# Residual kept with tokens on partitions from the convolution's output on

## The reference, cut to what matters

```python
for i in range(2):
    m = short_conv_mixer(x, ...) if i == 0 else dsa_mixer(x, ...)   # both end in  (...) @ w_out
    x = layer_norm(ALPHA * x + m, ln1_g[i], ln1_b[i])               # over the 1024 features of a token
    f = hier_moe(x, ...)     # top group, top 2 of 8 experts in it: 64 experts of 1024 x 256 (x2) and 256 x 1024
    x = layer_norm(ALPHA * x + f, ln2_g[i], ln2_b[i])
def layer_norm(x, g, b):
    mu = mean(x); var = mean(square(x - mu))
    return (x - mu) * rsqrt(var + 1e-5) * g + b
```

## Time and profile before

| what | value |
|---|---|
| three timed runs | 3143.69, 3145.0, 3147.49 us |
| the profiled execution | span 3143.2 us (the page gives the span and no other time for it) |
| PE, PEld busy | 2787.1 us (89%), 2133.7 us (68%) |
| DVE, ACT, POOL busy | 1063.2 us (34%), 707.9 us (23%), 108.9 us (3%) |
| chain that ended last | PE 70%, DMA 21%, DVE 4%, ACT 2% |
| HBM | 189 GB/s over the span |

### The profile page before, as it was taken

How to read it: one execution, slowest core, us unless ns; L and a number is a source line. 1 busy time by engine, 2 the same in 40 slices (tenths; PEclk the granted TensorE clock), 3 DMA queues, 4 the chain that set the end, 5 groups by cost and what they waited for, 6 DMA issues and landing times.

```text
span 3143.2 us, 51582 instructions
## 1 busy us (share of the span) xinstructions
PE 2787.1 (89%) x21208; PEld 2133.7 (68%) x21208; DVE 1063.2 (34%) x2168; ACT 707.9 (23%) x1224; POOL 108.9 (3%) x175
## 2 busy tenths in 40 slices
PE   6999999999899999996887887889999868878787
PEld 6888874755688888875666666754577656666666
DVE  4554642222522254435211111229155341111113
ACT  3212330143322243212100000112264310000012
POOL 0000001000000000000000000000000000000000
PEclk8999999999999999996999999989999879999998
DMA  6655333211223222320499999641100209999980
GB/s 229 190 184 184 134 103 107 81 54 54 81 84 104 94 93 80 108 94 1 196 422 422 422 422 422 255 152 52 67 1 27 81 27 400 422 422 422 422 369 27
DMA packets 205503, 590.07 MB, mean 188 GB/s; under 512 B 9264, under 2 KB 133360, under 8 KB 156000
## 3 DMA queue, kind: packets, MB, share of 16 engines
q1 hardware_dynamic: 202832, 575.47, 47.7%
q0 software_dynamic: 2288, 12.39, 1.2%
q10 hardware_dynamic: 288, 0.89, 0.1%
HBM read 586.58 MB, written 7.38 MB: 189 GB/s over the span
## 4 chain that ended last, share of the span: by engine, by line
PE 70%; DMA 21%; DVE 4%; ACT 2%; issue 2%; SPq 1%; DVEq 0%; ACTq 0%
PE bank L1638 33%; DMA ring<-in_exp_w 20%; PE bank L1945 8%; PE bank L2020 4%; PE bank L1791 4%; PE bank L1760 3%; PE bank L1919 2%; PE bank L2005 2%; PE bank L1597 2%; PE bank L1749 1%; PE bank L1578 1%; SPq L453 1%; PE bank L1839 1%; PE bank L1612 1%; PE bank L2109 1%
## 5 line engine op out<-in xcount | busy, mean ns | idle before, releaser
L1638 PE MATMUL bank<-parts 128*128 128x512 f32 x3008 | 937.3, 393 | 29.4 <-DVE parts L998 17.3
L1638 PEld LDWEIGHTS bank<-parts 128*128 128x128 f32 x3008 | 566.9, 190 | 149.3 <-issue 28.9
L1945 PE MATMUL bank<-ring,arena 128*64 128x256 f32 x4096 | 496.6, 393 | 178.8 <-DMA ring<-in_exp_w 178.1
L1638 PE MATMUL bank<-parts,ring_low 128*128 128x512 f32 x1504 | 588.6, 391 | 0.0
L1945 PEld LDWEIGHTS bank<-ring,arena 128*64 128x64 f32 x4096 | 329.4, 135 | 309.4 <-issue 203.6
L1638 PEld LDWEIGHTS bank<-parts,ring_low 128*128 128x128 f32 x1504 | 284.8, 189 | 59.9
L992 DVE TENSOR_TENSOR ring_low<-ring,parts 128x2048 fp32r<-128x2048 f32 x96 | 215.2, 2245 | 196.5 <-ACT parts L645 196.2
L1963 PEld LDWEIGHTS bank<-arena,ring 128*64 128x64 f32 x8192 | 266.2, 138 | 16.4 <-ACT arena L623 1.1
L1407 DVE SCALAR_TENSOR_TENSOR arena<-arena,bank 128x128 f32<-128x128 f32 x128 | 44.2, 346 | 656.3 <-ACT arena L765 656.3
L1963 PE MATMUL bank<-arena,ring 128*64 128x64 f32 x8192 | 263.3, 222 | 0.7 <-ACT arena L623 0.7
L645 ACT ACTIVATE parts<-ring 128x2048 fp32r<-128x2048 f32 x96 | 179.9, 1873 | 233.9 <-DMA ring<-in_w_ffn_in 109.3
(11 more groups left out here) (290 smaller groups left out, 2467.0 us busy)
## 6 DMA issues: line engine op xcount, KB each, us to landing
ring<-in_exp_w SPq DMA_DIRECT2D x384, 1024.0 KB, 10.3
ring<-in_w_ffn_in SPq DMA_DIRECT2D x44, 1024.0 KB, 5.9
ring<-in_w_ada SPq DMA_DIRECT2D x36, 1024.0 KB, 5.3
ring<-in_w_ffn_out SPq DMA_DIRECT2D x20, 1024.0 KB, 5.1
ring<-in_w_in SPq DMA_DIRECT2D x18, 1024.0 KB, 5.1
ring<-in_conv_w_in SPq DMA_DIRECT2D x12, 1024.0 KB, 5.1
ring<-in_attn_w_in SPq DMA_DIRECT2D x10, 1024.0 KB, 9.6
ring<-in_attn_w_out SPq DMA_DIRECT2D x8, 1024.0 KB, 5.0
```

The costliest lines, as they stand in the source:

```text
L1638: i = mm(o, a[:, cols[0], cols[1]], b, start=first_ and n == 0, stop=last_ and n == 2)
L1945: x = mm(bank[s][64 * f:64 * f + 64, 0:2 * P].rearrange("p (w n) -> p w n", w=2), XW[:, s, k], ring[:, 3 * s:3 * s + 2, c0:c0 + 2 * P - 1: ...
```

## The change

From the output product of the convolution on, the residual is `HT`, the same memory as `H` but read as `[128 tokens, 4 token tiles, 1024 features]`.

- **Residual turned.** During the convolution PE transposes `U` into two spare banks, four transposes after each of the 8 convolution tiles (`residual`), and ACT copies each group into `HT`.
- **Output products** (`token_output`, for `conv_out` and `dsa_out`): the activation tile is now the stationary operand and 512 columns of the weight the moving one. PE waits for whole chunks. In the second half the last two chunks are taken together, for one token tile after the other, so that bank `4 + t` is finished for `t = 0..3`.
- **Slot sum**: `SWT` stationary, the slot results moving; 4 token tiles for each half of the features.
- **Layer norm** by token tile on DVE (`bn_stats` on each half of 512, `bn_aggr`, reciprocal, one subtract-and-multiply over 1024) and ACT (root). Then PE turns the tile back to features (`turn_tokens`), and ACT and DVE apply gain and bias while they copy it out of the banks into `U` (`lifted`). The router's logits follow for each tile. The old products with ones, the squares, `to_tokens` and their waits are gone.
- **Gain and bias of the residual itself** are applied later, by POOL: `HT * g` and `+ b` over `[128, 1024]`, eight instructions after the last expert window, or in the attention's projections; rows `g` and `b` are broadcast over partitions by DMAs of POOL. The gather carries them for the experts in ACT's copy (`Identity` with scale and bias).
- **Low part `XTL`**: four instructions of 1024, placed after the router's weights and before the wait for the ranks.
- **Fourth layer norm**: DVE applies gain and bias itself and SP stores each token tile by its own DMA.

```diff
+            for d in range(KT):                                   # ACT, in the convolution
...
+                if d:
+                    residual(d - 1)
...
+            residual(7)
             out_high("conv_out", KT, lambda k: BC[:, k], UP, lambda k: conv_ready(k))
...
+            def token_output(name, kts, x, turn, logits):         # PE
+                def product(half, c, k, t):
...
+                        last = mm(bank[4 * half + t][:], a[:, at, P * t:P * t + P], b[:, k - 4 * c, :],
+                                  start=(k == m == 0), stop=(k == kts - 1 and m == 2))
+                for half, c in [(0, c) for c in range(n)] + [(1, c) for c in range(n - 2)]:
+                    ready(half, c)
...
+                for c in (n - 2, n - 1):
+                    ready(1, c)
+                for t in range(TT):
+                    for c in (n - 2, n - 1):
...
+                    if t >= 1:
+                        turn(t - 1)
+                    if t >= 2:
+                        logits(t - 2)
+                logits(2)
+                turn(3)
+                logits(3)
...
+                def tokens_back(half, t):                         # PE, slot sum
+                    if half:
+                        pe.wait_ge(sem("ht"), 8 * (1 + 2 * l) + t + 1)
+                    for s in range(8):
+                        for j, part in enumerate((YSH, YSL)):
+                            x = mm(bank[4 + t][:], SWT[:, s, P * t:P * t + P], part[half][:, s],
...
+                for t in range(TT):
+                    tokens_back(1, t)
+                    if l == 0 and t:
+                        turn_tokens(1, t - 1)
...
+            def deep_add(j, t, half, src):                        # DVE
+                STT(out=h, in0=h, scalar=ALPHA, in1=src, op0=ALU.mult, op1=ALU.add).then_inc(sem("ht"), 1)
+                dve.wait_ge(sem("ht"), n)
+                st.did(nc.vector.bn_stats(BNS[:, t, 6 * half:6 * half + 6], h))
+            def normal(j, t):
+                dve.wait_ge(sem("sd"), 4 * j + t + 1)
+                seq(nc.vector.reciprocal(RS[:, t:t + 1], SD[:, t:t + 1]))
+                TSc(HT[:, t], HT[:, t], MV[:, t, 0:1], RS[:, t:t + 1], ALU.subtract, ALU.mult).then_inc(sem("xn"), 1)
+            def layer_norm(j, second_half):
+                for t in range(TT):
+                    second_half(t)
+                    moments(j, t)
+                    if j == 3:
...
+                        stored(j, t)
+                        continue
+                    if t:
+                        lifted(j, t - 1)
+                    normal(j, t)
+                if j < 3:
+                    lifted(j, 3)
...
+                for n, v in enumerate((layer, 2 + layer) + ((5, 7) if layer else ())):   # POOL, before the windows
+                    pool.dma_start(ROWS[:, n], lnrows[v].partition_broadcast(P)).then_inc(sem("ln_vectors"), 16)
...
+                pool.wait_ge(sem("ln_vectors"), 160 if layer else 64)                    # POOL, after them
+                for t in range(TT):
+                    st.did(pool.tensor_tensor(HT[:, t], HT[:, t], ROWS[:, 0], ALU.mult))
...
+                    pool.wait_ge(sem("ht"), 16)                   # POOL, layer 0
+                    pool.dma_start(ROW2, lnrows[4].partition_broadcast(P)).then_inc(sem("ln_vectors"), 16)
                     pool.dma_start(BKT[0:BUCKETS], ...)           # and rel_bias, scratch, spread, TOE as before
...
+                    pool.wait_ge(sem("ln_vectors"), 80)
+                    pool.wait_ge(sem("lt"), 16)
+                    for t in range(TT):
+                        st.did(pool.tensor_tensor(HT[:, t], HT[:, t], ROW2, ALU.mult))
+                    st.wait()
+                    pool.dma_start(ROW2, lnrows[6].partition_broadcast(P)).then_inc(sem("ln_vectors"), 16)
+                    pool.wait_ge(sem("ln_vectors"), 96)
+                    for t in range(TT):
+                        pool.tensor_tensor(HT[:, t], HT[:, t], ROW2, ALU.add).then_inc(sem("resid"), 1)
...
-            out_low("dsa_out", HEADS2, lambda k: Q2[:, k], UP, lambda: deep_out("dsa_out", 4, 0))
-            deep_out("dsa_out", 4, 1)
-            norm(6, 3, lambda k: col("ln1_g", 8 + k))
+            dve.wait_ge(sem("resid"), 8)
+            out_low("dsa_out", HEADS2, lambda k: Q2[:, k], UP, lambda: deep_out("dsa_out", 4, 2, 0), half_at=6)
+            layer_norm(2, lambda t: deep_out("dsa_out", 4, 2, 1, (t,)))
...
+            for t in range(TT):
+                sp.wait_ge(sem("final"), t + 1)
+                sp.dma_start(out[0, P * t:P * t + P], HT[:, t]).then_inc(sem("stored"), 16)
```

More of the change, by code:

```diff
@@ L757, in moe @@
                     c, k = g // 8, g % 8
-                    evac(XST[:, k, 512 * c:512 * c + 512], bank[g % 4][:], "moe_xst")
+                    A_(XST[:, k, 512 * c:512 * c + 512], bank[g % 4][:], ACT.Identity, scale=gpart[:, l, k:k + 1],
+                       bias=gpart[:, 2 + l, k:k + 1]).then_inc(sem("moe_xst"), 1)
                 act.wait_ge(sem("moe_plan"), l + 1)
@@ L853, in _ @@
             weights_high(split_at["ffn1"] + 1)
[L854 removed]
+            norm(2, lambda k: mod[:, 48 + k:49 + k], True)
             ffn(1)
@@ L865, in conv_ready, with residual @@
                     act.wait_ge(sem("conv_b"), 8)
+            def residual(g):
+                act.wait_ge(sem("side_tp"), g + 2)
+                evac(HT[:, g // 2, 512 * (g % 2):512 * (g % 2) + 512], bank[6 + g % 2][:], "side_out")
             for d in range(KT):
@@ L1027, in roots, with norm @@
                     TSc(diag[:, t], ident, small[:, 52 + t:53 + t], None, ALU.mult).then_inc(sem("diag"), 1)
-            def norm(i, ln, gain, parts_of=None, shift=None):
-                if ln:
-                    dve.wait_ge(sem("mean"), ln)
-                    for k in range(KT):
-                        STT(out=H[:, k], in0=bank[2][:], scalar=-1.0 / D, in1=H[:, k],
-                            op0=ALU.mult, op1=ALU.add).then_inc(sem("centred"), 1)
+            def norm(i, gain, parts_of=None, shift=None):
                 if i:
@@ L1266, in _, with deep_out @@
                     weights_low(split_at["conv"] + 3 * (d // 2 + 1) + 2)
[L1267 to L1274 removed]
+            def deep_out(name, n, j, half, tiles=range(TT)):
+                for t in tiles:
+                    bank_ready(name, n, half, t)
+                    deep_add(j, t, half, bank[4 * half + t][:])
+            out_low("conv_out", KT, lambda k: BC[:, k], UP, lambda: None)
+            dve.wait_ge(sem("side_out"), 9)
+            deep_out("conv_out", 2, 0, 0)
+            layer_norm(0, lambda t: deep_out("conv_out", 2, 0, 1, (t,)))
             def moe(l):
[L1277 to L1279 removed]
                 dve.wait_ge(sem("rows"), 16 * 12)
@@ L1437, in moe, with token_half @@
                     rest(g)
-                for d in range(KT):
-                    if d < 4:
-                        rest(8 + 2 * d)
-                        rest(9 + 2 * d)
-                    dve.wait_ge(sem("moe_f"), 8 * l + d + 1)
-                    deep_add(d, bank[4 + d % 4][:])
+                def token_half(t, half):
+                    dve.wait_ge(sem("moe_f"), 8 * l + 4 * half + t + 1)
+                    deep_add(1 + 2 * l, t, half, bank[4 + t][:])
+                for t in range(TT):
+                    rest(8 + 2 * t)
+                    rest(9 + 2 * t)
+                    dve.wait_ge(sem("resid"), 8 * l + t + 1)
+                    token_half(t, 0)
+                layer_norm(1 + 2 * l, lambda t: token_half(t, 1))
             moe(0)
-            norm(5, 2, lambda k: col("ln2_g", k))
             dve.wait_ge(sem("vb_mm"), 1)
@@ L1606, in rstd, with norm @@
                 x.then_inc(sem("rstd"), 1)
-            def norm(i, ln):
-                if ln:
-                    for k in range(KT):
-                        pe.wait_ge(sem("h"), 8 * (i - 1) + max(k + 1, 4))
-                        x = mm(bank[2][:], ones[:], H[:, k], start=(k == 0), stop=(k == KT - 1))
-                    x.then_inc(sem("mean"), 1)
-                for k in range(KT) if ln else range(5, KT):
+            def norm(i):
+                for k in range(5, KT):
                     sums(i, k, k == 0, "squares", 8 * (i - 1) + k + 1)
@@ new lines, in turn_tokens @@
+            def turn_tokens(j, t):
+                pe.wait_ge(sem("xn"), 4 * j + t + 1)
+                if j == 1 and t >= 2:
+                    pe.wait_ge(sem("u_low"), 4 * j + t - 1)
+                    pe.wait_ge(sem("u_high"), 4 * j + t - 1)
+                for h in range(2):
+                    for k in range(4):
+                        x = tp(turned_banks(j, t)[h][:, P * k:P * k + P], HT[:, t, P * (4 * h + k):P * (4 * h + k) + P], ident)
+                    x.then_inc(sem("lt"), 1)
@@ L1719, in _, with logits_of @@
+            def logits_of(l, t):
+                pe.wait_ge(sem("u_low"), 8 * l + t + 1)
+                pe.wait_ge(sem("u_high"), 8 * l + t + 1)
```

(16 more changed lines are left out.)

280 lines of the change are left out of this document (159 added, 121 removed).

## The result

The changed kernel takes 3054.7 us (median of 4 runs, 3051.9 to 3057.5) against 3146.2 us before (4 runs, 3143.7 to 3147.5): ratio 0.971, 95% interval 0.9697 to 0.9724, faster by 91.5 us where 105.9 were forecast. That lies in the predicted range of 3026 to 3060, 15.6 us above the predicted 3039.1 (which starts from 3145.0, the median of three runs), and outside the forecast's own narrower range of 3031 to 3046. By the spans of the profiled executions it is 3143.2 to 3050.1, -93.1 us against the predicted -105.9.

What follows compares the result with a forecast made beforehand. Latency at four layer norms, 160.9 us with nothing at its limit, was taken as what the change works on; -26.9 - 21.5 - 24.9 - 33.0 + 0.4 = -105.9 us from 3145.0 gave 3039.1, own range 3031 to 3046, wider range 3026 to 3060.

Steps and rivals of the forecast that it cites:

- Norm 1: Layer norm between the convolution's output product and the router: shorter exposed tail less added transposes, turns and starting wait, net -26.9 us.
- Norm 2: Layer norm between layer 0's slot sum and the attention's projections: shorter tail, clock gain and POOL contention, net -21.5 us.
- So I count half of what that cost as gained: Projections' first stretch after norm 2: shorter PE rest recovers half the half-clock cost, 1.8 us, less something: -1.4 us.
- The contention with POOL: POOL's four residual additions may hold up DVE's key chain in the attention: between 0 and 8 us, 2 taken.
- Norm 3: Layer norm after the attention's output product: shorter tail less inline turns, starting wait and a new stall, net -24.9 us.
- The stall: Attention's output product: PE waits because chunk 7's tiles share buffers with chunk 5; +3.1 us, between 1.5 and 5.
- Norm 4: Layer norm after the last slot sum: DVE the slower engine at 4.45 us a tile, then a quarter store; -33.0 us.
- `XTL`, 4 x 1.28 = 5.1 us, fits the 5.11 us wait: Low-part subtractions after the router hide in the wait for the ranks: 0 to +0.6 us a layer, 0.1 taken.
- (d): Rival: swapped-operand matmuls in output products and slot sums run at 0.43 us for 0.228, slower at 3207; chance 0.03.
- (c): Rival: memory-paced expert stages swallow gains ahead of them, only norms 2 and 4 pay, 3090; chance 0.04.
- (a): Rival: the tile-wise tails run on PE's half clock, norms 1 and 3 lose 14 us, 3056; chance 0.12.
- (b): Rival: POOL's additions hold the key chain all 8 us and `bn_stats` is near its upper price, 3048; chance 0.12.

Runs made afterwards that it cites:

- run 4: Changed kernel with three PE waits loosened in the output products (first chunk tile by tile, last chunk later, last residual group turned earlier); 3041.3 us.
- Run 3: Changed kernel with PE turning tile 3 ahead of the logits of tile 2 in norms 1 and 3; 3047.5 us.
- run 6: Changed kernel with the bias table loaded earlier and one bias product done by PE ahead of norm 2's last turn; 3048.8 us.
- run 9: Changed kernel with the edits of run 2, Run 3, run 4, run 5 and run 6 together; 3034.5 us.
- run 10: As run 9, but XTH and XTL in the changed kernel's feature order, made by reading HT in order and writing with a 512-byte step; 3034.7 us.
- run 11: As run 9 but without the edit of run 5, so XTH and XTL are made as in the changed kernel; 3034.6 us.
- run 2: Changed kernel with POOL's arithmetic on the attention's residual moved behind DVE's key chain; 3054.9 us.
- run 12: Changed kernel with one wait loosened: PE waits for the last chunk only behind the first row's 12 products of the chunk before; 3048.9 us.
- Run 8: Changed kernel without norm 4's first scalar-tensor-tensor per tile (mean subtraction and gain), so the output is incomplete; 3052.3 us.
- run 1: Changed kernel with XTL's four subtractions reading and writing in natural order, leaving the low parts of the features misordered; 3050.3 us.
- run 7: The changed kernel measured again, unaltered; 3054.3 us.
- run 5: Changed kernel with XTH and XTL kept in HT's order and the gather's weight load reading with a step of 8 elements; 3054.3 us.

## Why the prediction was right, and where it was short

**Norm 1 (-26.9; measured -23.3).** Start and transposes came out as worked out (+5.6). Among the products it was +5.1 for +3.5: the forecast's own terms let PE rest 3.9 us at the start (ACT's copy 0.6, the first tile 1.5, three more tiles 1.8; 3.8 measured), though it calls 3 us the longest rest, and it charged only the rest, while the clock at half behind it cost another 1.5 (34.44 us against run 4's 32.93 for the same 144 matmuls). The tail was 10.9 for 8.7. The chain of steps was right; logits 2 waited for ACT's lifting to 3.45 us after E where I had PE free at 2.7 and took 2.01 for 1.78, the lifting of tile 3 took 1.5 for 1.25, and logits 3 ran partly at half clock (2.75 for 1.78). Run 3 reaches the figure with another order on PE: 8.8.

**Norm 2 (-21.5; -17.2).** The tail was 7.0 for 6.0, with the two bias products at half clock behind it (1.86 us the first, as before the change). "So I count half of what that cost as gained" is the step that failed in sign: PE's rest before the turn of tile 3 was the 3 us that the forecast had, but the clock fell behind it (0.50 from 2029 to 2038), and the projections' first stretch took 9.86 us for 9.02; the part costs +0.8 instead of -1.4. Nor did a rest of 2.0 us there keep the clock up (runs 6 and 9 to 11). The contention with POOL was foreseen as a mechanism with bounds 0 and 8; 2 were taken, 3.8 measured, and run 2 shows it is this. DVE's L1582, 4 elements a partition, took 1.95 us and the first of the four L1584 2.28 for 0.24: both end as one of POOL's four instructions ends (2074.51 + 3 x 2.31 = 2081.4, and 2083.7), while copies from the banks and the reduction just before ran at their usual length beside POOL. The Trainium skill, "SBUF — State Buffer", section "Who interferes with whom", says that a tensor-scalar in a two-port mode and a GpSimd instruction that reads SBUF exclude each other for the whole instruction, and that a reduction doesn't take part. The trace agrees with that rule; that L1582 and L1584 run in such a mode is not shown. The "some 4 us" that the prediction gave by that page was the better figure.

**Norm 3 (-24.9; -23.6).** The stall stood at 3.1 us between 1.5 and 5 and measured 3.3; it is the buffers of chunk 7, as argued: ACT's first copy into them starts at 2409.04, as PE's last product before the rest ends (2409.02), and runs 4 and 12 cover the wait with products. What the forecast lacked is the stall's second price: 4.3 to 6.5 us more in stage and tail together where the clock falls behind it, in five of the eight profiles that have the rest. The median of 3054.7 may lie above the profiled execution (3051.9) for that reason: over the run its granted clock is 0.971, in the three longer ones 0.967 to 0.969. It is not shown where these lost it, since only one execution in each set has a trace.

**Norm 4 (-33.0; -34.5).** DVE is the bound: 4.28 us a tile (4.45 predicted), store 2.6 us (2.9). Run 8 confirms the queue. The tail itself is -33.8; the other 0.6 lie ahead of E and are not explained.

**What was costed at nothing.** POOL's eight instructions behind the last window ended at 1983.2, 11 us ahead of the first tile's slot sum, as foreseen. "`XTL`, 4 x 1.28 = 5.1 us, fits the 5.11 us wait": this term was mis-sized. The four took 7.9 us, because they read `HT` with a step of 32 bytes; with no step 4.6 (run 1). The price came from a row of the same shape but not of the same access. With 5.2 us for 0.2 it is 5.0 of the 12.8 us that are missing, the largest part, and no rival had it. The Trainium skill states in "SBUF — State Buffer", section "Specifications (TRN2)", that SBUF has 16-byte lines and wants two hits on a line for full bandwidth. A step of 32 bytes has one hit a line; the trace agrees in direction, and the page gives no size. Here it is +67% on DVE's subtraction (a median of 2.04 us for 1.22), +74% on the weight load and +100% on ACT's copy (2.14 for 1.07). With a step of 512 bytes it is +57% on the subtraction (write and one read) and +89% on ACT's copy (write alone, 2.02).

**The rivals.** (d), the swapped form of matmul, is excluded: 0.228 to 0.235 us each at the full clock. (c) as well: from the gather to the end of the slot sum it is the old length plus 1.8. (a) held in part: the clock fell ahead of norm 1's product, late in its tail, in norm 2, and in norm 3 in some executions. (b) held for POOL and not for `bn_stats` (0.69). Its 3048 and (a)'s 3056 enclose the result, but neither explains it: the 12.8 us are `XTL` 5.0, clock 3.7 (norm 1's product 1.5, the projections 2.2), POOL 1.8, and 2.3 of the rest, in which the three tails of norms 1 to 3 stand with 4.7, about 1 of that from the half clock in logits 3 of norm 1. So the mechanism held, and that the range held is in part luck: its width was made for the clock and for POOL, and `XTL`, which it left out, took a quarter of the 21 us between the forecast and the upper end. One execution of the unaltered kernel in run 7 took 3059.3 us, 0.7 below the upper end.

## What to carry to other kernels

A layer norm between large products costs what its latency exposes. Dealt out over tiles behind the products still running, 161 us became 37 (10.9, 7.0, 10.15 and 9.4); 30 of the 123 gained were paid elsewhere. What is left depends on the order on PE at the last tile and on how fine the waits are. Where a transposing reorder is moved, price it by its step in bytes and not by its shape; and price a rest of PE twice, once for its length and once for the clock behind it. Tiny DVE instructions on a critical chain shouldn't stand beside two-input work of POOL, whose place in time is free.

## What the runs showed of the hardware

- A rest of PE of 3.3 us was followed by half the clock in five of eight profiles and not in three, in kernels with the same work there; rests of 0.6 us (runs 4 and 9 to 12) and, ahead of norm 1's product, 1.6 us (runs 4 and 9 to 11) were not. The rest of 3.8 us ahead of norm 1's product was, in all nine profiles that have it, and so were in norm 2 the 3.0 us in all nine and the 2.0 us in all four (runs 6 and 9 to 11), where small products stand around the rest. The eight sets of runs with the 3.3 us spread over 3.9 to 9.9 us, the five without it over 1.6 to 4.5; that the one causes the other is not shown.
- DVE, subtraction of 128x1024 fp32: 1.22 us contiguous, 1.97 to 2.06 with a 32-byte step in one read, 1.91 with a 512-byte step in the write and one read (run 10; which of the two costs it is not separated). ACT's copy of the same shape took 1.07 us contiguous (run 5), 2.14 with a 32-byte step in the read and 2.02 with a 512-byte step in the write alone.
- A DVE tensor-scalar of 4 elements a partition took 0.18 us alone and 0.45 to 1.95 us beside POOL's two-input instructions of 2.3 us.
- PE's weight load of 128x128 fp32: 0.188 us contiguous, 0.327 with a 32-byte step; hidden but for 0.015 us a matmul.
- `bn_stats` of 512 fp32: 0.69 us, `bn_aggr` of two such 0.21. POOL's two-input instruction of 128x1024 fp32: 2.3 to 2.4 us.
